# Trainium2, two transformer blocks on one core: expert routing in fewer chunks, gates spread over 48 chunks, the conditioning row in groups of column tiles

## The reference, cut to what matters

```python
def peer_ffn(h, w_q, sub_keys, u_tab, v_tab):
    scores = jnp.einsum('bshpd,hpkd->bshpk', q, sub_keys)        # 8 heads x 2 x 128 keys
    s1, i1 = lax.top_k(scores[..., 0, :], 16)
    s2, i2 = lax.top_k(scores[..., 1, :], 16)
    cand_s = (s1[..., :, None] + s2[..., None, :]).reshape(B, S, 8, 256)
    top_s, top_pos = lax.top_k(cand_s, 16)
    ids = jnp.take_along_axis(cand_id, top_pos, axis=-1)         # i1 * 128 + i2
    gate = jax.nn.softmax(top_s, axis=-1)
    # then, for each token: sum over its picks of gate * gelu(u[id] . h) * v[id]

mod = (silu(c) @ w_ada[i] + b_ada[i])     # the conditioning row: 1024 -> 6 * 1024
```

## Time and profile before

| | before |
|---|---|
| device time, median of 3 runs | 2864.71 us (2859.34 to 2865.49) |
| the profiled execution, its own time | 2864.54 us |
| its span (first to last instruction) | 2862.8 us |
| PE busy | 2486.0 us (87%) |
| DVE busy | 1885.8 us (66%) |
| ACT busy | 1203.6 us (42%) |
| POOL busy | 338.3 us (12%) |
| DMA, mean | 174 GB/s |
| mean granted clock of TensorE | 0.928 of full |

### The profile page before, as it was taken

How to read it: one execution, slowest core, us unless ns; L and a number is a source line. 1 busy time by engine, 2 the same in 40 slices (tenths; PEclk the granted TensorE clock), 3 DMA queues, 4 the chain that set the end, 5 groups by cost and what they waited for, 6 DMA issues and landing times. The chain is left out here.

```text
span 2862.8 us, 45532 instructions
## 1 busy us (share of the span) xinstructions
PE 2486.0 (87%) x15092; PEld 2074.3 (72%) x15092; DVE 1885.8 (66%) x3336; ACT 1203.6 (42%) x1854; POOL 338.3 (12%) x298
## 2 busy tenths in 40 slices
PE   6977897588596789999889999577799998899997
PEld 6634843377244789998878888475799998788886
DVE  5653564255773478878966777555488879777666
ACT  4321422044321344465544544253244565554454
POOL 0000000000320000000033443010000000044333
PEclk9987998689898899999999999797899999999999
DMA  6331642354452367765467777622277664477775
GB/s 184 131 118 59 190 140 88 89 183 141 147 177 94 105 197 228 227 219 166 132 212 242 240 241 242 179 89 88 95 228 228 218 219 144 144 239 242 242 240 175
DMA packets 278073, 498.23 MB, mean 174 GB/s; under 512 B 70088, under 2 KB 146120, under 8 KB 277984
## 3 DMA queue, kind: packets, MB, share of 16 engines
q1 hardware_dynamic: 264928, 494.93, 54.2%
q10 hardware_dynamic: 13056, 2.15, 0.5%
HBM read 462.35 MB, written 34.65 MB: 174 GB/s over the span
## 5 line engine op out<-in xcount | busy, mean ns | idle before, releaser
L2238 PE MATMUL psum<-split_operands 128*128 128x512 f32 x3072 | 701.7, 391 | 13.4 <-ACT split_operands L2196 13.4
L2238 PEld LDWEIGHTS psum<-split_operands 128*128 128x128 f32 x3072 | 580.1, 189 | 134.5 <-ACT split_operands L2196 13.7
L1958 PE MATMUL psum<-split_operands 128*128 128x256 f32 x4096 | 542.5, 286 | 20.0 <-ACT split_operands L1993 19.9
L1958 PEld LDWEIGHTS psum<-split_operands 128*128 128x128 f32 x4096 | 511.5, 193 | 24.1 <-issue 10.1
L2209 DVE TENSOR_TENSOR split_operands<-weights_ring,split_operands 128x1024 fp32r<-128x1024 f32 x256 | 316.9, 1238 | 209.6 <-ACT split_operands L2196 209.6
L2183 POOL TENSOR_TENSOR arena<-arena,residual_gates 128x256 f32 (+1 forms) x256 | 284.3, 1111 | 1269.6 <-DMA residual_gates<-expert_activations 1269.6
L2196 ACT CAST split_operands<-weights_ring 128x1024 fp32r<-128x1024 f32 x256 | 269.4, 1052 | 350.2 <-PE psum L2238 347.4
L2036 DVE TENSOR_TENSOR split_operands<-weights_ring,split_operands 128x1024 fp32r<-128x1024 f32 x256 | 313.1, 1223 | 108.9 <-ACT split_operands L1993 108.5
L257 PE MATMUL psum<-split_operands 128*128 128x256 f32 x2304 | 290.3, 290 | 42.4 <-DVE split_operands L280 42.4
L257 PEld LDWEIGHTS psum<-split_operands 128*128 128x128 f32 x2304 | 288.4, 199 | 45.2 <-DVE split_operands L287 42.7
L1962 PE MATMUL psum<-split_operands 128*128 128x256 f32 x2048 | 287.4, 283 | 0.0
(11 more groups left out here) (303 smaller groups left out, 2393.3 us busy)
## 6 DMA issues: line engine op xcount, KB each, us to landing
weights_ring<-in_peer_u_dram SPq DMA_DIRECT2D x256, 512.0 KB, 3.7
weights_ring<-in_peer_v_dram SPq DMA_DIRECT2D x256, 512.0 KB, 4.4
weights_ring<-in_w_ada_dram SPq DMA_DIRECT2D x48, 1024.0 KB, 5.2
expert_activations<-residual_gates SPq DMA_DIRECT2D x256, 128.0 KB, 2.0
residual_gates<-expert_activations SPq DMA_DIRECT2D x256, 128.0 KB, 4.0
weights_ring<-in_w_in_dram SPq DMA_DIRECT2D x6, 2048.0 KB, 8.0
weights_ring<-in_hg_w_in_dram SPq DMA_DIRECT2D x5, 2048.0 KB, 7.9
arena<-in_hg_w_in_dram SPq DMA_DIRECT2D x5, 2048.0 KB, 7.9
```

The costliest lines, as they stand in the source:

```text
L1958: nc.tensor.matmul(K.ps[:, 4 + b, 0:SEQ], u_t[:, b, 0, k], h[:, wh, k], start=(k == 0 and wh == 0), stop=False)
L2238: last = nc.tensor.matmul(K.ps[:, 4 + 2 * t + half], g[:, s, w, t * P:(t + 1) * P], vs[:, b, wv, half * 512:(half + 1) * 512], start=(star ...
```

## The change

**Routing.** The four-dimensional operations over a quarter of the heads replace those over one head: the candidates are added by 4 instructions of 1024 elements (16 of 256 before). The comparison and the multiplication, on 16-bit floats now, are 16 instructions of 1024 elements for each layer in place of 64 of 256. The ramp comes from a constant tile, so GpSimd's iota goes. `PACE` is 1560; an f16 element counts half.

**Gates.** `ROUTED` falls from 96 to 80 and `EXP_AT` from 68 to 64. The 64 groups are built over 48 chunks, in a turn of three chunks with 1, 1 and 2 groups. The loop body holds 12 chunks and 16 groups (before 4 chunks and 8 groups). ACT keeps the groups of a chunk beside the next one, as before.

**Conditioning row.** A slot now holds one block of 128 input rows by 3 or 4 pieces of 512 columns (768 KB or 1024 KB), where it held 4 blocks by one piece (1024 KB). Successive products so go to different column tiles of PE: `tile_position` changes with every product, where it changed every eight. `stage_mixers` has 16 slots (12 before), and its calls of `mod.pe` are cut differently.

```diff
@@ ModulationProducts
     def load(self, sp, first, last):
+        width = self.group * 512
         for m in range(first, last):
             if m >= 2:
                 sp.wait_ge(self.w_used, m - 1)
-            src = self.K.i["w_ada_2"][self.l, (m % 2) * 512:(m % 2 + 1) * 512,
-                                      bass.ds(self.n0 * 512 + (m // 2) * 512, 512)]
-            sp.dma_start(self.ring[:, m % 2], src.rearrange("(k p) n -> p k n", p=P)
-                         ).then_inc(self.w_loaded[m % 2], 16)
+            k, r = m % KD, m // KD
+            src = self.K.i["w_ada_2"][self.l, k * P:(k + 1) * P, bass.ds(self.n0 * 512 + r * width, width)]
+            sp.dma_start(self.ring[:, m % 2], src).then_inc(self.w_loaded[m % 2], 16)
...
         for m in range(first, last):
+            k, r = m % KD, m // KD
             pe.wait_ge(self.w_loaded[m % 2], 16 * (m // 2 + 1))
-            for k in range(KD // 2):
-                kk = (m % 2) * (KD // 2) + k
-                ins = self.K.nc.tensor.matmul(self.out(m // 2), self.c[:, kk:kk + 1], self.ring[:, m % 2, k],
-                                              start=(kk == 0), stop=(kk == KD - 1),
-                                              tile_position=(0, 32 * (m // 2 % 4)))
+            for q in range(self.group):
+                ins = self.K.nc.tensor.matmul(self.out(r * self.group + q), self.c[:, k:k + 1],
+                                              self.ring[:, m % 2, q * 512:(q + 1) * 512],
+                                              start=(k == 0), stop=(k == KD - 1), tile_position=(0, 32 * q))
             ins.then_inc(self.w_used, 1)
@@ stage_mixers
-            mod.load(sp, 2, 12)
+            mod.load(sp, 2, 16)
...
-            mod.pe(pe, 6, 10)
+            mod.pe(pe, 6, 11)
...
-            mod.pe(pe, 10, 12)
+            mod.pe(pe, 11, 16)
@@
-ROUTED = NKEYS - GROUPS // 2
-EXP_AT = 68
+ROUTED = 80
+BESIDE = [[4 * q + r for r in part] for q in range(4) for part in ((0,), (1,), (2, 3))]
+BUILT = 16
+EXP_AT = 64
 SELECT_AT = ROUTED - SLOTS
-PACE = 1500
+PACE = 1560
@@
+def gated_chunks(engine, body):
+    def turn(i, early):
+        for u, groups in enumerate(BESIDE):
+            body(i * len(BESIDE) + (ROUTED + u), u % SLOTS, [(i * BUILT + o, o) for o in groups], early)
+    turn(0, True)
+    with engine.Fori(1, (NKEYS - ROUTED) // len(BESIDE)) as i:
+        turn(i, False)
@@ stage_expert_inputs, vector
+            rows = G // 4 * TOPK
...
-                link(nc.vector.tensor_copy(partf, part))
-                for g in range(G):
-                    ins = nc.vector.tensor_tensor(onehot[:, g], partf[:, g].unsqueeze(2).broadcast_to([P, TOPK, TOPK]),
-                                                  rampb, ALU.is_equal)
...
-                    pace(TOPK * TOPK)
+                link(nc.vector.tensor_copy(parth, part.rearrange("p g k -> p (g k)").unsqueeze(2).broadcast_to(
+                    [P, G * TOPK, 2])))
+                for q, gs in enumerate(quarters):
+                    ins = nc.vector.tensor_tensor(
+                        onehot[:, gs].rearrange("p g k (a w) -> p (g k) a w", w=2), rampb,
+                        parth[:, q * rows:(q + 1) * rows].unsqueeze(2).broadcast_to([P, rows, TOPK // 2, 2]),
+                        ALU.is_equal)
...
+                    pace(rows * TOPK // 2)
...
-            def chunk(n, s, early):
+            def chunk_and_gates(n, s, groups, early):
                 low(n, s, False)
-                for r in range(2):
-                    g = 2 * (n - ROUTED) + r
-                    weights.hot(dve, g, r, early)
-                    weights.parts(dve, g, r)
+                for g, o in groups:
+                    weights.hot(dve, g, o % 2, early)
+                    weights.parts(dve, g, o % 2)
```

More of the change, by code:

```diff
@@ L443, with __init__ @@
 class ModulationProducts:
-    def __init__(self, K, sem, area, row_area, l, n0, blocks, banks):
-        self.K, self.l, self.n0, self.blocks, self.banks = K, l, n0, blocks, banks
+    def __init__(self, K, sem, area, row_area, l, n0, rounds, group, banks):
+        self.K, self.l, self.n0, self.rounds, self.group, self.banks = K, l, n0, rounds, group, banks
+        self.blocks, self.slots = rounds * group, rounds * KD
         self.c = area.take(KD)
-        self.row = row_area.take(len(banks), 512)
-        self.ring = K.ring[:].rearrange("p (s k n) -> p s k n", s=2, k=KD // 2)
+        self.row = row_area.take(rounds, 512)
+        self.ring = K.ring[:, 0:2 * group * 512].rearrange("p (s n) -> p s n", s=2)
         self.c_loaded, self.c_ready = sem("c_loaded"), sem("c_ready")
@@ L474, in out @@
     def out(self, q):
-        part, bank = 32 * (q % 4), self.banks[q // 4]
+        part, bank = 32 * (q % self.group), self.banks[q // self.group]
         return self.K.ps[part:part + 1, bank]
@@ L500, in store @@
         for q in range(self.blocks):
-            part = 32 * (q % 4)
+            part = 32 * (q % self.group)
             dst = self.K.mod_dram[self.l:self.l + 1, bass.ds(self.n0 * 512 + q * 512, 512)]
-            sp.dma_start(dst, self.row[part:part + 1, q // 4]).then_inc(self.stored, 16)
+            sp.dma_start(dst, self.row[part:part + 1, q // self.group]).then_inc(self.stored, 16)
         sp.wait_ge(self.stored, 16 * self.blocks)
@@ L1789, in pipeline @@
 def pipeline(engine, first, last, unroll, body, straight=True):
-    start = first // unroll
     if straight:
@@ L1795, in pipeline @@
             body(first + u, u, True)
-        start += 1
-    with engine.Fori(start, last // unroll) as i:
+    with engine.Fori(1 if straight else 0, (last - first) // unroll) as i:
         for u in range(unroll):
-            body(i * unroll + u, u, False)
+            body(i * unroll + (first + u), u, False)
+def gated_chunks(engine, body):
[5 more added lines that the diff above has]
+        turn(i, False)
 SLOTS = 4
@@ L1943, in _ @@
                 sp.wait_ge(a_stored[s], NKEYS // SLOTS * 16)
-        @block.gpsimd
-        def _(pool):
-            nc.gpsimd.iota(ramp16, pattern=[[1, TOPK]], base=0, channel_multiplier=0,
-                           allow_small_or_imprecise_dtypes=True).then_inc(ramp_ready, 1)
         @block.tensor
@@ L2005, in chunk, with chunk_and_gates @@
                     gelu(n - 1, (s - 1) % SLOTS, early)
-            def chunk_and_gates(n, s, early):
+            def chunk_and_gates(n, s, groups, early):
                 chunk(n, s, False)
-                if not early or n > ROUTED:
-                    for r in range(2):
-                        weights.keep(act, 2 * (n - 1 - ROUTED) + r, 2 * ((s + 1) % 2) + r)
+                first, o0 = groups[0]
+                for back in range(len(BESIDE[TURN.index(o0) - 1]), 0, -1):
+                    if not early or o0 > 0:
+                        weights.keep(act, first - back, (o0 - back) % 4)
             nc.scalar.copy(h[:, 0], K.h_t[:]).then_inc(h_high, 1)
@@ L2107, in _ @@
                         link(ins)
-                    pace(TOPK * TOPK)
-                for q in range(4):
-                    gs = slice(q * G // 4, (q + 1) * G // 4)
+                    pace(rows * TOPK // 2)
+                for q, gs in enumerate(quarters):
                     link(nc.vector.tensor_reduce(picked[:, w, gs].rearrange("p g k -> p (g k)"),
                                                  onehot[:, gs].rearrange("p g k a -> p (g k) a"), AX.X, ALU.add))
-                    pace(G // 4 * TOPK * TOPK)
+                    pace(rows * TOPK)
```

65 lines of the change are left out of this document (34 added, 31 removed).

## The result

| | before | after |
|---|---|---|
| device time, median | 2865.1 us (2859.3 to 2870.1) | 2794.2 us (2791.3 to 2798.7) |
| ratio, 95% interval | | 0.9755 [0.973, 0.9779] |
| span of the profiled execution | 2862.8 us | 2796.9 us |
| PE busy | 2486.0 us (87%) | 2388.3 us (85%) |
| mean granted clock | 0.928 | 0.913 |

The changed kernel is faster by 70.9 us. Forecast were 62.6 less, 2802 us, with a range of 2778 to 2836. Two later sets of runs of the same kernel gave 2795.3 and 2790.2 us.

What follows compares the result with a forecast made beforehand. In the expert inputs PE was taken as the bound for the first 96 chunks, DVE from there on. The sum was 2864.5 - 43.6 (gates) - 19 (conditioning row) = 2802 us, range 2778 to 2836.

Steps and rivals of the forecast that it cites:

- Gates over 48 chunks: Expert inputs: three-chunk turns of 10.5 us, PE's bound being 10.38; -21.8 us a stage, -44 in both.
- Unshifted DVE (11.14): Rival, expert inputs: DVE's work can't shift between a turn's chunks; turn 11.14 us, gates -23, total 2822 us; chance 0.12.
- Shorter routing at 0: Expert inputs: the shorter routing gives nothing by itself, as PE is the bound beside it; 0 us.
- Conditioning row: Mixers and both HGRN2 stages: products on successive column tiles partly overlap on PE; -19 us together.
- half overlap: Conditioning row: one product's second pass lies beside the next's first, halving time; 1.3 us a slot of three.
- the lower clock's price: Mixers: after idle stretches PE's next slots, transposes and scores run at half speed; some 4 us.
- Mixers: Conditioning row in both mixers: pieces sum to -6, the lower clock takes some 4; -2 us in each.
- HGRN2 gates: Conditioning row there: ACT's copies could start 8.5 to 10 us earlier, the lower clock takes a part; -6 us.
- HGRN2 attention: Conditioning row there: the last levels' shorter products take most of DVE's waits for PE; -9 us.
- No overlap: Rival, conditioning row: column tiles don't overlap; HGRN2 stages 0, mixers +10 us, total 2831 us; chance 0.25.
- draining: Rival, conditioning row: every column-tile change drains PE, 0.16 us each, 27 us; 2858 us at the most; chance 0.02.
- Full overlap at full clock: Rival, conditioning row: column tiles overlap fully at full clock; -37 us, total 2784 us; chance 0.09.

Runs made afterwards that it cites:

- e1: The changed kernel with the conditioning row as in the kernel before, so routing and gates alone: 2823.0 us, ratio 0.9855 to the kernel before.
- e6: The changed kernel with PE multiplying only the high part of each gate, the low part left out: 2775.6 us, ratio 0.9684.
- e3: The changed kernel with the routing's operations as before and PACE 1800: 2797.7 us, ratio 0.9765.
- e4: The changed kernel with a slot's four products on one column tile and four banks in both HGRN2 stages: 2811.2 us, ratio 0.9811.
- e7: The changed kernel with only the first two slots of each conditioning row loaded and used again: 2763.6 us, ratio 0.9637.
- e2: The kernel before with the new conditioning row alone: 2835.7 us, ratio 0.99.
- a0: The changed kernel run once more, unchanged: 2795.3 us, ratio 0.9749.
- a1: The changed kernel run a third time, unchanged: 2790.2 us, ratio 0.9741.
- e8: The changed kernel with GpSimd in HGRN2 attention waiting until DVE takes scores from PSUM: 2792.6 us, ratio 0.9751.
- e5: The changed kernel with conditioning-row slots 11 and 12 moved ahead of the second projection in the mixers: 2784.3 us, ratio 0.9709.

## Why the prediction was right, and where its steps were off

**Gates over 48 chunks: right.** -21.8 us a stage were forecast, -20.8 and -19.7 came, and e1 puts both stages at -42 against -43.6. The mechanism (PE as the bound, DVE's work shifted between the chunks of a turn) is shown by the rows without waits and by e6. The mis-sized term is a group on PE: "Its two groups took 0.87 us where nothing held them up (1301.82 to 1302.69), 0.435 each". A group costs 0.50 us, two cost 0.95, so the turn is 2 x 3.38 + 3.83 = 10.59 where I had 10.38 as the bound. The missing 0.07 us are in the product that follows: it takes 2.15 us behind a group and 2.08 otherwise, and both numbers stood in the earlier trace rows. The prediction summed the group alone. The choice of 10.5 covered 0.12 of these 0.21 us a turn.

**Unshifted DVE (11.14): wrong rival.** DVE waits only 0.54 us a turn, and PE never waits for the gates' tiles, where it waited 28.4 us in both layers before.

**Shorter routing at 0: right**, by e3. It freed what it should: an f16 operation of 1024 elements took 0.687 us where I had taken 0.75.

Shortest, median and longest in ns, then first and last start:

```profile
L2112 DVE TENSOR_TENSOR arena<-ramp_half,arena x16: 684/687/693, 1164.0 to 2211.1; 128x1024 f16<-128x1024 f16 x16
```

**Conditioning row: right sign, step wrong.** The step that failed is "the two passes of one product use the same columns, and PE works in order; so I expect only the second pass of one product to lie beside the first of the next". The row at 145.62 shows a slot of three at 1.03 us, against my 1.3; at the lower clock it is 1.88. Three products with two passes each run as if they were one: by 145.7 three passes have started, the other three start at 146.05, and two slots (1.89 us for 12 passes) are four such steps. The order within a product, from which I argued, didn't hold the other tiles back. e4 shows it from the other side.
The Trainium skill's figure in "TensorE: Matmul & The Clock Gate", the section on the measured speedup against the span model, is 2.38 times for three column tiles. Here it is 2.64 / 1.03 = 2.6 times for one slot, and 13.2 / 4.47 = 3.0 times for the five slots in a row of e7, so the trace lies above the Trainium skill's figure, and further above my half overlap.

**The places of the row.** The sum was -19, and e2 measured -29. The term that was mis-sized most is the lower clock's price, and not the slot's 1.3 us, which matters little where PE waits for loads.

- Mixers. The piece inside the up-projection gave 4.2 us where I had 4.3. The transposes start 9.7 us earlier in the stage (10.3 in the second layer) where the terms say 11.3. The piece ahead of the scores took 13.6 us, from 178.21 to 191.78, where I had 13: +6.2 us against the kernel before, for +5.5.
- The clock in the mixers. I took 4 us for it from a sum of -6, and -3.5 and -4.0 leave 2.3 and 1.8. The projection was slow already in the kernel before (3.23 us, at 183.77) and is not now (1.96), which makes up for the slower transposes. The 1.7 us more of the scores cost nothing: the next scores start at 202.10, where they started at 204.56, and that is still 3.5 us earlier in the stage.
- HGRN2 gates. I had 8.5 to 10 us less a part for the clock, so 6, and 8.8 came. ACT's copies reach DVE's end in spite of a mean granted clock of 0.59, where it was 0.90.
- HGRN2 attention. It gave 5.9 us in the execution of the table, 6.1 in a0 and 10.7 in a1. I had 9, which lies within this scatter.

In the total the row's 10 us too little stand against 2 us too much for the gates, so that 8 us are left.

**What I had not seen.** Two things hold time back now. The loads and the lower clock behind them hold 32 us together by e7; that this is why the row gave 29 and not the 37 of the full overlap is argued, not measured. The other is GpSimd against DVE in the attention, which e8 shows; how much of the stage it costs isn't settled, since in no run was it absent. DVE's busy time in the stage rose from 96.5 to 99.9 us, so the change added 3.4 us there at most in this execution.

**Rivals.** "No overlap" and "draining" fall with the 1.03 us. The 0.16 us of the draining rival were a misreading besides: the 600 ns are the mean length of a pass and the 440 ns the distance of two starts. A pass is 590 to 592 ns long in most cases in both kernels. "Full overlap at full clock" had the overlap right and the clock wrong. Its 2784 us lie 10 us from the result, on the other side than the forecast, so 0.09 was little for it: I had the Trainium skill's figure and no row against it, and chose the middle. In the bounds, two stages at 10.38 give -47, not -48; nothing hangs on it.

Not explained is the 3 us between the two expert input stages. The stretch is 618.8 to 620.2 us in every other run, with the old routing and with the old row too, and 622.2 in the one trace of the kernel before.

## What to carry to other kernels

- Products with one output row, put on different column tiles one right after another, cost almost the time of one (three: 0.89 us a slot in e7, against 0.88 for one product). After that ask for their loads: with two buffers PE waited here, its granted clock fell to 0.50, and the products that followed took 3.78 us instead of 2.05.
- Place such pieces where PE stands idle anyway and early enough that their buffers come free: moving two slots ahead of a wait gave 11 us in e5 for two lines.
- When a small product is put into a stream, price it by the distance of the stream's starts with and without it, not by its own length. And when two engines tie (10.59 and 10.05 us), expect the second as soon as the first is relieved.

## What the hardware showed that I had not expected

DVE's operation on two SBUF operands of 1024 f32 elements takes 1.21 us, and up to 3.1 us while GpSimd runs one of the same kind; GpSimd's take 2.9 to 3.0 then, some longer still, instead of 1.9 to 2.1. Beside DVE's taking of scores from PSUM (2.75 us with and without) neither is slower. 3.07 is about 1.21 + 1.9, as if the two took turns.
The Trainium skill has this in "SBUF — State Buffer", section "Who interferes with whom": an exclusive lock on the read port that the two engines share, for a DVE operation with two SBUF inputs. The trace agrees, and the forecast had no term for it.
